# Layer passages of a two-model transformer kernel: turned input evicted ahead of the next weight rounding, and the first slot's products in the order of the input tiles

## The chip, the cores and the metric

One core of a Trainium2 chip. The metric is device time in microseconds for one launch. The kernel before took 2083.91 us, the median of three runs (2080.11 to 2088.32).

## What is computed

Two small models, one after the other, on a sequence of 512 positions of width 1024, in float32. Cut to what matters:

```python
# first model, depth 2 (layer 0: state space mixer; layer 1: sparse attention, "DSA")
x = x + mixer(rmsnorm(x, norm_mix[i]))
x = x + (silu(gate) * up) @ w_down          # gate, up = rmsnorm(x, norm_ffn[i]) @ w_gate_up, width 2816
# DSA: proj = h @ w_in; indexer scores; top 128 keys per query; softmax over them; @ w_o
# second model, depth 1
x = x + hybrid_mixer(rmsnorm(x, g_mix))     # @ w_in ("HIN"), four head groups, group norms, @ w_out ("HOUT")
x = x + cross_attention(rmsnorm(x, g_cross), rmsnorm(mem, g_mem))   # @ w_q ("XQ"), @ w_kv ("MEM"), @ w_o ("XO")
x = x + square(relu(rmsnorm(x, g_mlp) @ w_up)) @ w_down             # "MLP", width 4096
return rmsnorm(x, g_final)
```

## The kernel before

**Number format.** Every product of a layer is made of three matmuls in fp32r (`three`, L1812 to 1817): weights and inputs are split into a rounded part and a rest, and hi x hi, lo x hi, hi x lo are added. An input tile has a `xT_hi` (written by ScalarE) and a `xT_lo` (VectorE, PSUM minus hi).

**Weights** come in 147 slots of 2048 columns, in two buffers each. SP loads `raw` (`slot_free(g)` waits until slot g-2 is split), ScalarE rounds it to `w_hi` (`round_slot`, L824 to 828: waits for the load and for `w_used`, slot g-2 used up), POOL subtracts to `w_lo` (`split_rest`, L571 to 573), and TensorE waits for `w_split` before its slot.

**Two kinds of slot on TensorE.** `t_slot` (L1839) makes two output tiles of 128 columns in two PSUM banks, 2 x 8 input tiles x 3 = 48 matmuls, with the turned input as the moving operand of 512. Before, all eight input tiles go into the first output tile (then `t_first`), and all eight into the second (then `w_used`). `n_slot` (L1819) makes rows by 512 columns: four row blocks `tb` in banks 4 to 7, four input tiles each. Its user `panel` (L1910) waits for a number of `xT_lo` before each row block: 5, 6, 7, 8 where eight banks are used for turning, 4 where four are.

**Layer passages.** Between two layers the residual is finished row block by row block: VectorE adds the panel (`add_panel`), ScalarE squares, POOL makes the inverse root (`norm_rstd`), VectorE writes the left half of `x_n`, ScalarE the right half (`norm_sq`). TensorE turns `x_n` into the eight banks (`turn_normed`, L1867; bank k holds input tile k), ScalarE evicts to `xT_hi` (`turn_hi`, L815), VectorE makes `xT_lo` (`turn_lo`, L1366). The order on ScalarE is its program order: squares and `x_n`, then `round_run` of the next layer's *second* slot (L880, 898, 1085, 1143, 1153), then `turn_hi`. There are six such passages: into the first FFN (`turn_normed(0)`), DSA (1), second FFN (2), HIN (3), XQ (4) and MLP (5). `ffn_act` (L883) ends with the rounding, and `turn_hi` for DSA and HIN stands behind its call.

Where the input is not normed (WO after the DSA attention, MEM, HOUT), `turn_rows` (L1853) turns it with four banks 0 to 3: from the fifth tile on TensorE waits for the `xT_lo` four tiles back.

**Around the attention of DSA.** VectorE picks the top 128 keys (`choose_rounds`, `choose`, L1516 to 1542; each block counts up `idx_chosen`) and then starts the attention. POOL, when its head work is done, splits the first WO slot (L663) and then makes the inverse sums (`invert_sums`, L654), one per unit of attention.

## Time and profile before

| | |
|---|---|
| Median of three runs | 2083.91 us |
| The profiled execution, its time | 2082.05 us |
| Its span | 2080.20 us |
| TensorE busy | 1963.1 us (94%) |
| ScalarE, VectorE, POOL busy | 761.0, 738.5, 844.9 us (37%, 35%, 41%) |
| Mean granted TensorE clock | 0.971 |

In the profile PE is TensorE's matmuls and PEld its weight loads, DVE is VectorE, ACT ScalarE, SP the engine that issues loads. A timeline row gives the start, the time from start to end (of several instructions in a row, where x is over 1), the engine, the line, the instruction with output and inputs, and in brackets how long the engine had stood idle and what ended that. Matmuls overlap: one lasts 0.39 us while the next starts 0.227 us after it at full clock, so their spacing is read from the starts. The granted clock is in shares of 2.4 GHz; its two levels are 1.2 and 2.4 GHz, and a value between them is a stretch with both.

### The profile page before, as it was taken

How to read it: one execution, taken by the hardware profiler on the slowest of the kernel's cores; microseconds unless marked ns; L12 is line 12 of the kernel's file. 1: busy time of each engine (PE TensorE's matmuls, PEld its weight loads, DVE VectorE, ACT ScalarE, POOL GpSimd, SP SyncE). 2: the span in 40 equal slices, each digit the busy share in tenths (PEclk: the TensorE clock that was granted, in tenths of full speed). 3: DMA queues.
4: the chain of work that ended last, by engine and by line, in shares of the span. 5: the costliest groups of instructions: out<-in, count | busy, mean ns of one | idle time of the engine just before them, and what ended most of it. 6: DMA issues, size and time to landing. Idle time of an engine off the chain costs nothing.

```text
span 2080.2 us, 25333 instructions
## 1 busy us (share of the span) xinstructions
PE 1963.1 (94%) x9587; PEld 1602.7 (77%) x9587; DVE 738.5 (35%) x1279; ACT 761.0 (37%) x1233; POOL 844.9 (41%) x416
## 2 busy tenths in 40 slices
PE   2998999999998999899999999999997989999998
PEld 1777878888887878678788888878776867888887
DVE  7973231111003388852211110010158245702631
ACT  5533242322123244673332221242476353212212
POOL 1003434443444448643343443444442433443443
PEclk8799999999999899999999999999998999999999
DMA  5113323333232212101233323343300312333321
GB/s 121 18 24 127 101 81 95 87 100 91 91 101 67 81 61 82 41 22 42 81 100 101 101 80 102 103 137 95 98 22 3 110 41 70 92 102 101 100 88 75
DMA packets 210344, 168.20 MB, mean 81 GB/s; under 512 B 19537, under 2 KB 175641, under 8 KB 210200
## 3 DMA queue, kind: packets, MB, share of 16 engines
q1 hardware_dynamic: 207392, 163.10, 26.9%
q10 hardware_dynamic: 2872, 4.04, 0.6%
q8 instruction: 50, 0.82, 0.2%
q14 instruction: 30, 0.25, 0.0%
HBM read 162.63 MB, written 2.13 MB: 79 GB/s over the span
## 4 chain that ended last, share of the span: by engine, by line
PE 61%; issue 21%; POOL 8%; DVE 7%; ACT 3%; SPq 0%; DMA 0%; POOLq 0%; ACTq 0%; DVEq 0%
PE PS L1815 48%; POOL w_lo L573 7%; PE PS L1994 4%; PE PS L1978 2%; PE PS L1985 2%; ACT w_hi L828 1%; DVE stay L1591 1%; PE PS L1719 1%; PE PS L1720 1%; PE PS L1740 1%; PE PS L1752 1%; DVE o_nat L1637 0%; POOL head_rs L560 0%; DVE ranked L1526 0%; PE PS L1760 0%
## 5 line engine op out<-in xcount | busy, mean ns | idle before, releaser
L573 POOL TENSOR_TENSOR w_lo<-raw,w_hi 128x2048 fp32r<-128x2048 f32 x147 | 680.6, 4630 | 1006.7 <-ACT w_hi L828 1006.7
L828 ACT ACTIVATE w_hi<-raw 128x2048 fp32r<-128x2048 f32 x147 | 281.4, 1914 | 679.1 <-PE PS L1815 679.1
L1815 PE MATMUL PS<-xT_hi,w_hi 128*128 128x512 f32 x1104 | 432.0, 391 | 9.1 <-DVE xT_lo L1376 9.1
L1815 PE MATMUL PS<-xT_hi,w_lo 128*128 128x512 f32 x1104 | 431.7, 391 | 0.0
L1815 PE MATMUL PS<-xT_lo,w_hi 128*128 128x512 f32 x1104 | 431.4, 391 | 0.0
L1815 PEld LDWEIGHTS PS<-xT_hi,w_hi 128*128 128x128 f32 x1104 | 208.5, 189 | 53.6 <-issue 6.7
L1815 PEld LDWEIGHTS PS<-xT_lo,w_hi 128*128 128x128 f32 x1104 | 208.5, 189 | 43.6
L1815 PE MATMUL PS<-w_hi,hT_hi 128*128 128x512 f32 x608 | 237.1, 390 | 5.1 <-POOL w_lo L573 5.1
L1815 PE MATMUL PS<-w_hi,xT_hi 128*128 128x512 f32 (+2 forms) x592 | 232.3, 392 | 9.9 <-issue 4.6
L1815 PEld LDWEIGHTS PS<-xT_hi,w_lo 128*128 128x128 f32 x1104 | 208.3, 189 | 43.0
L1815 PE MATMUL PS<-w_lo,hT_hi 128*128 128x512 f32 x608 | 236.6, 389 | 0.0
L1815 PE MATMUL PS<-w_hi,hT_lo 128*128 128x512 f32 x608 | 236.6, 389 | 0.0
L1815 PE MATMUL PS<-w_hi,xT_lo 128*128 128x512 f32 (+2 forms) x592 | 230.3, 389 | 0.0
L1815 PE MATMUL PS<-w_lo,xT_hi 128*128 128x512 f32 (+2 forms) x592 | 230.2, 389 | 0.0
L1417 DVE TENSOR_TENSOR x_res<-x_res,PS 128x512 f32<-128x512 f32 x48 | 32.9, 686 | 440.8 <-PE PS L1815 440.8
L1429 DVE TENSOR_TENSOR gbuf<-gbuf,PS 128x512 f32<-128x512 f32 x44 | 30.3, 688 | 385.1 <-PE PS L1815 385.1
L1815 PEld LDWEIGHTS PS<-w_hi,xT_hi 128*128 128x128 f32 x592 | 115.8, 196 | 35.3 <-issue 9.6
L1815 PEld LDWEIGHTS PS<-w_hi,hT_hi 128*128 128x128 f32 x608 | 114.1, 188 | 30.4 <-POOL w_lo L573 6.8
L1815 PEld LDWEIGHTS PS<-w_hi,hT_lo 128*128 128x128 f32 x608 | 114.1, 188 | 23.8
L1815 PEld LDWEIGHTS PS<-w_lo,hT_hi 128*128 128x128 f32 x608 | 114.1, 188 | 23.6
L1815 PEld LDWEIGHTS PS<-w_hi,xT_lo 128*128 128x128 f32 x592 | 115.5, 195 | 21.4
L1815 PEld LDWEIGHTS PS<-w_lo,xT_hi 128*128 128x128 f32 x592 | 115.9, 196 | 20.8
(322 smaller groups left out, 2200.7 us busy)
## 6 DMA issues: line engine op xcount, KB each, us to landing
raw<-in_ffn_w_gate_up SPq DMA_DIRECT2D x88, 512.0 KB, 4.9
raw<-in_ffn_w_down SPq DMA_DIRECT2D x40, 512.0 KB, 4.5
raw<-in_w_up SPq DMA_DIRECT2D x32, 512.0 KB, 4.8
raw<-in_w_down SPq DMA_DIRECT2D x32, 512.0 KB, 4.5
raw<-in_dsa_w_in SPq DMA_DIRECT2D x28, 512.0 KB, 4.2
raw<-in_w_in SPq DMA_DIRECT2D x21, 512.0 KB, 4.2
raw<-in_s_w_glu SPq DMA_DIRECT2D x16, 512.0 KB, 4.6
raw<-in_dsa_w_o SPq DMA_DIRECT2D x8, 512.0 KB, 4.3
```

The source lines that it names most:

```text
L573: pool.tensor_tensor(w_lo[:, par, :], raw[:, par, :], f32(w_hi[:, par, :]), ALU.subtract).then_inc(w_split, 1)
L828: act.activation(w_hi[:, par, :], raw[:, par, :], ACT.Copy).then_inc(w_rounded, 1)
L1417: tt(x_res[:, tb, cols], x_res[:, tb, cols], PS[:, 4 + tb, :], ALU.add).then_inc(n_free, 1)
L1429: tt(gbuf[:, pair, 1, :], gbuf[:, pair, 0, :], PS[:, 2 * pair + 1, :], ALU.mult).then_inc(t_free, 1)
L1591: dve.tensor_tensor_scan(rest[:, ::-1], rest[:, ::-1], one[:, 0:1].broadcast_to([P, cols]), 1.0, ALU.mult, ALU.mult).then_inc(at_max, 1)
L1719: mm(o, uT[:, GB * b + g, :], taps[:, g, :, :].rearrange("p t h -> p (t h)"), start=True, stop=False)
L1720: ins = mm(o, states[:, g, :], out_a[b % 3][:, g, 1:CH + 1, :].rearrange("p t h -> p (t h)"), start=False, stop=True)
L1740: mm(o, b_n[:, GB * b + g, :], out_a[b % 3][:, g, 0:CH, :].rearrange("p t h -> p (t h)"), start=g % 4 == 0, stop=False)
L1815: ins = mm(o, a if weights_stay else c, c if weights_stay else a, start=first and n == 0, stop=last and n == 2)
L1978: mm(PS[:, t % 4, 0:k.shape[1]], q[half:half + HD], k[half:half + HD], start=True, stop=True).then_inc(at_dot, 1)
L1985: ins = tr(PS[:, 4 + e % 2, P * j:P * j + P], logit[:, e % 4, P * j:P * j + P], ident[:, :])
L1994: ins = mm(PS[:, 6 + e % 2, 0:P], probT[:, e % 2, P * j:P * j + P], v[j], start=j == 0, stop=j == len(v) - 1)
```

## The change

It has four parts.

1. ScalarE: in all six passages `turn_hi` moves ahead of the `round_run` that stood before it.
2. TensorE, `t_slot` with turned input (the first slot of each t-layer, and, since it stands in a loop, every even slot of both FFNs and of the first MLP part; also HIN's, MEM's and XQ's first): input tile by input tile into both output tiles, so `t_first` comes one step before `w_used`. XQ uses banks 0 and 1 instead of 2 and 3, and its wait for three `xT_lo` goes; MEM waits for one tile more. `turn_normed` turns the left half of the last row block before it waits for the right half.
3. TensorE, panels with turned input (DSA, WO, HOUT): a new `n_slot_turned` goes in waves: with input tile m come row blocks 0 to m-1 for that tile, and row block m for all tiles so far. WO and HOUT turn with eight banks, starting at bank 4, and HOUT's turning waits for `vx` to be evicted. DSA's passage turns and evicts tiles 4 to 7 first (`UPPER_FIRST`), and its two weight slots are loaded in that order.
4. POOL waits for `idx_chosen` 3 before it splits the first WO slot.

```diff
@@ sync
-            panel_loads(DSA_SLOT, w_in[:, :, 3 * D:3 * D + 512], 512)
+            for j, k in enumerate((4, 0)):
+                slot_free(DSA_SLOT + j)
+                load_rows((DSA_SLOT + j) % 2, w_in[:, k:k + 4, 3 * D:3 * D + 512], 512)
@@ gpsimd
+            pool.wait_ge(idx_chosen, 3)
             split_run(WO_SLOT, 1)
@@ scalar
             norm_sq(0, glu_done, 4 * TB, slice(768, D))
+            turn_hi(KT, KT, gain=2, banks=8)
             round_run(9, 1)
-            turn_hi(KT, KT, gain=2, banks=8)
...
                 norm_sq(1 + 2 * layer, n_free, TB * (FFN_PANEL[layer] + 3))
+                turn_hi((2, 5)[layer] * KT, KT, gain=(1, 4)[layer], banks=8, order=(UPPER_FIRST, range(KT))[layer])
                 round_run(g0 + FT + 1 + 2 * len(FFN_DOWN), 1)
...
             attend_act(dsa_units, DSA_UNIT, late_slot=(40, WO_SLOT + 1))
-            turn_hi(3 * KT, KT)
+            turn_hi(3 * KT, KT, banks=8, at=4)
...
-            tiles_out(XQ_SLOT, XQ_TILE, qxT, HD ** -0.5)
+            tiles_out(XQ_SLOT, XQ_TILE, qxT, HD ** -0.5, pair=0)
@@ tensor, t_slot
-                for t in range(2):
-                    for k in range(KT):
-                        if turns is not None and t == 0:
-                            pe.wait_ge(x_lo_done, turns - KT + k + 1)
-                        at = step[0] * k + step[1] * t
...
-                    ins.then_inc(w_used if t else t_first, 1)
+                for k in range(KT):
+                    pe.wait_ge(x_lo_done, turns - KT + k + 1)
+                    tile(0, k)
+                    if k == 1:
+                        tile(1, 0)
+                    if k >= 1:
+                        tile(1, k)
+            def n_slot_turned(g, par, ni, ks, j0):
+
+                pe.wait_ge(w_split, g + 1)
+                for m in range(TB):
+                    pe.wait_ge(x_lo_done, j0 + m + 1)
+                    pe.wait_ge(n_free, ni * TB + m + 1)
+                    for tb, j in [(tb, m) for tb in range(m)] + [(m, j) for j in range(m + 1)]:
+                        cols = slice(512 * j, 512 * j + 512)
+                        ins = three(PS[:, 4 + tb, :], w_hi[:, par, cols], w_lo[:, par, cols],
+                                    xT_hi[:, ks[j], P * tb:P * tb + P], xT_lo[:, ks[j], P * tb:P * tb + P], False, j == 0, False)
+                ins.then_inc(w_used, 1)
@@ tensor, turn_rows
-                    if k >= 4:
-                        pe.wait_ge(x_lo_done, j0 + k - 3)
+                    if k >= banks:
+                        pe.wait_ge(x_lo_done, j0 + k - banks + 1)
@@ tensor, turn_normed
+                for tb in range(TB - 1):
+                    left(tb)
+                pe.wait_ge(norm_right, TB * n + TB - 1)
+                for k in range(4, 7):
+                    for tb in range(TB - 1):
+                        turn(k, tb)
+                if not upper_first:
+                    left(TB - 1)
+                pe.wait_ge(norm_right, TB * n + TB)
                 for k in range(4, 7):
                     turn(k, TB - 1)
-                for t in range(TB):
-                    turn(7, t)
+                for tb in range(TB):
+                    turn(7, tb)
+                if upper_first:
+                    left(TB - 1)
@@ tensor, program
-            turn_rows(3 * KT, KT, o_nat)
-            for j in range(2):
-                panel(WO_SLOT + 2 * j, WO_PANEL + j, turns=(3 * KT, None)[j])
+            turn_rows(3 * KT, KT, o_nat, banks=8, at=4)
+            panel_turned(WO_SLOT, WO_PANEL, 3 * KT)
+            panel(WO_SLOT + 2, WO_PANEL + 1)
...
-            pe.wait_ge(x_lo_done, 6 * KT + 4 + 2 * (MEM_TILE % 2) + 1)
+            pe.wait_ge(x_lo_done, 6 * KT + 4 + 2 * (MEM_TILE % 2) + 2)
...
+            pe.wait_ge(n_free, TB * (MEM_PANEL + 2))
             pe.wait_ge(grp_norm, TB)
...
-            pe.wait_ge(x_lo_done, 8 * KT + 2 * (XQ_TILE % 2) + 1)
-            t_slot(XQ_SLOT, XQ_SLOT % 2, XQ_TILE, XQ_TILE % 2, xT_hi, xT_lo, turns=9 * KT)
+            t_slot(XQ_SLOT, XQ_SLOT % 2, XQ_TILE, 0, xT_hi, xT_lo, turns=9 * KT)
```

## Rows read from the trace of the kernel before

**Rows 1.** page, part 1: busy us of each engine (share of the span) xinstructions
```profile
PE 1963.1 (94%) x9587; PEld 1602.7 (77%) x9587; DVE 738.5 (35%) x1279; ACT 761.0 (37%) x1233; POOL 844.9 (41%) x416
```

**Rows 2.** TensorE's waits: us in total, times, longest us
```profile
PE PS L1815 <- DVE xT_lo L1376: 10.6, 5, 3.2
...
PE PS L1985 <- ACT logit L1048: 9.0, 2, 8.0
```

**Rows 3.** timeline, second FFN's passage: start us, us, engine, line, instruction [idle before]
```profile
992.59 2.40 PE L1870 MATMUL PS<-ident,x_n 128*128 128x128 f32 x20 [0.26 <-ACT x_n L854]
...
993.57 1.90 ACT L828 ACTIVATE w_hi<-raw 128x2048 fp32r<-128x2048 f32 x1
...
995.38 4.71 ACT L821 ACTIVATE xT_hi<-PS,gains 128x512 fp32r<-128x512 f32 x8
...
995.55 4.57 POOL L573 TENSOR_TENSOR w_lo<-raw,w_hi 128x2048 fp32r<-128x2048 f32 x1 [2.64 <-ACT w_hi L828]
...
996.07 5.36 DVE L1376 SCALAR_TENSOR_TENSOR xT_lo<-PS,gains,xT_hi 128x512 fp32r<-128x512 f32 x8 [2.64 <-ACT xT_hi L821]
...
996.97 0.62 PE L1815 MATMUL PS<-xT_hi,w_hi 128*128 128x512 f32 x1 [1.98 <-DVE xT_lo L1376]
...
1000.69 0.39 PE L1815 MATMUL PS<-xT_hi,w_hi 128*128 128x512 f32 x1
```

**Rows 4.** the same view, passage into DSA
```profile
641.92 0.73 ACT L854 ACTIVATE x_n<-x_res,rstd 128x512 f32<-128x512 f32 x1 [0.41 <-POOL rstd L586]
...
648.54 0.47 PE L1815 MATMUL PS<-w_hi,xT_hi 128*128 128x512 f32 x1 [4.57 <-issue]
```

**Rows 5.** the same view, passage into the WO panel
```profile
942.36 1.73 PEld L1859 LDWEIGHTS PS<-ident,o_nat 128*128 128x128 f32 x16 [0.57 <-DVE o_nat L1608]
...
946.63 0.48 PE L1815 MATMUL PS<-w_hi,xT_hi 128*128 128x512 f32 x1
```

**Rows 6.** the same view, passages into first FFN, HIN, HOUT (two), XQ and MLP
```profile
271.85 5.28 PE L1870 MATMUL PS<-ident,x_n 128*128 128x128 f32 x24 [0.62 <-DVE x_n L1386]
...
1367.63 0.47 PE L1815 MATMUL PS<-xT_hi,w_hi 128*128 128x512 f32 x1 [1.99 <-DVE xT_lo L1376]
...
1611.61 4.21 PEld L1859 LDWEIGHTS PS<-ident,o_nat 128*128 128x128 f32 x24 [3.45 <-issue]
...
1617.16 0.48 PE L1815 MATMUL PS<-w_hi,xT_hi 128*128 128x512 f32 x1
...
1668.73 0.50 PE L1815 MATMUL PS<-xT_hi,w_hi 128*128 128x512 f32 x1 [3.20 <-DVE xT_lo L1376]
...
1718.43 2.81 PE L1870 MATMUL PS<-ident,x_n 128*128 128x128 f32 x24 [0.93 <-DVE x_n L1386]
```

**Rows 7.** the same view, end of top-k and start of the attention
```profile
845.40 4.51 POOL L573 TENSOR_TENSOR w_lo<-raw,w_hi 128x2048 fp32r<-128x2048 f32 x1
...
845.79 4.40 DVE L1535 TENSOR_SCALAR ranked<-score,top 128x512 f32<-128x512 f32 x1
...
850.95 0.49 DVE L1537 TENSOR_SCALAR equal<-score,top 128x512 f32<-128x512 f32 x1
...
856.12 2.08 POOL L661 TENSOR_TENSOR inv_sum<-row_sum,minus_one 128x1 f32<-128x1 f32 x4 [6.22 <-ACT logit L1048]
...
858.24 0.28 DVE L1608 TENSOR_SCALAR o_nat<-PS,inv_sum 128x64 f32<-128x64 f32 x1 [0.48 <-PE PS L1994]
```

**Rows 8.** the same view, XO slot: first and last of 24 matmuls
```profile
1710.84 0.39 PE L1815 MATMUL PS<-w_hi,xT_hi 128*128 128x512 f32 x1
...
1716.06 0.39 PE L1815 MATMUL PS<-w_hi,xT_lo 128*128 128x512 f32 x1
```

**Rows 9.** stretches: us, busy us of five engines (x), PEclk (granted clock), DMA, GB/s
```profile
995.00:1000.00 5.00, 3.03 (x8) 2.40 (x9) 3.93 (x6) 5.00 (x9) 4.45 (x1) 0.71 0.01 3
...
1367.00:1372.00 5.00, 4.37 (x19) 3.67 (x20) 5.00 (x8) 3.74 (x7) 3.80 (x1) 1.00 0.02 3
```

**Rows 10.** one line's instructions: duration ns min/median/max, first and last start us, form
```profile
L1637 DVE TENSOR_TENSOR o_nat<-o_nat,rstd x4: 1219/1223/5592, 1602.5 to 1605.9; 128x1024 f32<-128x1024 f32 x4
```

More of the change, by code:

```diff
@@ L813, in _, with turn_hi @@
             states_out(NB - 1)
-            def turn_hi(j0, n, gain=None, width=S, dst=xT_hi, view=None, banks=4, k0=0):
-                for k in range(k0, n):
-                    act.wait_ge(turned, j0 + k + 1)
-                    o, i = dst[:, k, 0:width], PS[:, k % banks, 0:width]
+            def turn_hi(j0, n, gain=None, width=S, dst=xT_hi, view=None, banks=4, k0=0, order=range(KT), at=0):
+                for n_th in range(k0, n):
+                    k = order[n_th]
+                    act.wait_ge(turned, j0 + n_th + 1)
+                    o, i = dst[:, k, 0:width], PS[:, (k + at) % banks, 0:width]
                     if view:
@@ L1364, in _, with turn_lo @@
                     output_map(b + 2)
-            def turn_lo(j0, n, gain=None, width=S, hi=xT_hi, lo=xT_lo, view=None, banks=4):
-                for k in range(n):
-                    dve.wait_ge(x_hi_done, j0 + k + 1)
-                    o, h, i = lo[:, k, 0:width], f32(hi[:, k, 0:width]), PS[:, k % banks, 0:width]
+            def turn_lo(j0, n, gain=None, width=S, hi=xT_hi, lo=xT_lo, view=None, banks=4, order=range(KT), at=0):
+                for n_th in range(n):
+                    k = order[n_th]
+                    dve.wait_ge(x_hi_done, j0 + n_th + 1)
+                    o, h, i = lo[:, k, 0:width], f32(hi[:, k, 0:width]), PS[:, (k + at) % banks, 0:width]
                     if view:
@@ L1440, in _ @@
             ffn_dve(0)
-            turn_lo(2 * KT, KT, gain=1, banks=8)
+            turn_lo(2 * KT, KT, gain=1, banks=8, order=UPPER_FIRST)
             dve.wait_ge(ld_qk, 16 * 4)
@@ L1853, in turn_rows, with tile @@
-            def turn_rows(j0, n, src, tbs=TB):
+                def tile(t, k):
+                    at = step[0] * k + step[1] * t
+                    cols = slice(at, at + P)
+                    ins = three(PS[:, 2 * pair + t, 0:width], w_hi[:, par, cols], w_lo[:, par, cols],
+                                hi[:, k, 0:width], lo[:, k, 0:width], True, k == 0, k == KT - 1)
+                    if k == KT - 1:
+                        ins.then_inc(w_used if t else t_first, 1)
+                if turns is None:
+                    for t in range(2):
+                        for k in range(KT):
+                            tile(t, k)
+                    return
@@ L1872, in turn, with left @@
                         ins.then_inc(turned, 1)
-                for tb in range(TB):
+                def left(tb):
                     pe.wait_ge(norm_left, TB * n + tb + 1)
@@ L1906, in _, with panel, panel_turned @@
             ffn_pe(0, 2 * KT)
-            turn_normed(1, 2 * KT)
-            def panel(g0, ni, n=512, turns=None, banks=4, after=None):
+            turn_normed(1, upper_first=True)
+            def panel(g0, ni, n=512, after=None):
                 for k in range(2):
-                    need = [turns + min(KT, (4 + 4 * k if banks == 4 else 5 + tb + 4 * k)) for tb in range(TB)] if turns is not None else None
-                    n_slot(g0 + k, (g0 + k) % 2, ni, range(4 * k, 4 * k + 4), xT_hi, xT_lo, k == 0, k == 1, n, turns=need, after=after)
+                    n_slot(g0 + k, (g0 + k) % 2, ni, range(4 * k, 4 * k + 4), xT_hi, xT_lo, k == 0, k == 1, n, after=after)
+            def panel_turned(g0, ni, j0, order=range(KT)):
+                n_slot_turned(g0, g0 % 2, ni, order[0:4], j0)
+                n_slot(g0 + 1, (g0 + 1) % 2, ni, order[4:KT], xT_hi, xT_lo, False, True, turns=[j0 + KT] * TB)
             def turn_heads(pi):
```

51 lines of the change are left out of this document (22 added, 29 removed).

## The prediction

> **What bounds the kernel now.** I read the page first: TensorE is busy 94% of the span, no other engine over 41% [rows 1]. The layers' inner loops are therefore bound by matmuls, which the change leaves alone. Time can only come from the holes in TensorE's row. The list of its waits shows which holes the change touches: five waits for `xT_lo`, together 10.6 us, and one of 8.0 us for the first softmax exponent [rows 2]. Then I read the timeline of each layer passage, since the list hides what stood behind each wait.
>
> Rows 3 are the pattern (the passage into the second FFN). TensorE turns the last block of rows, 20 transposes from 992.59 in 2.40 us. ScalarE meanwhile rounds the *next* weight slot (`w_hi`, 1.90 us), and only at 995.38 begins to evict the turned tiles. VectorE follows at 996.07 with `xT_lo`, 8 tiles in 5.36 us or 0.67 each, and TensorE starts at 996.97 on the first one. The rounded slot is needed one whole slot later: 48 matmuls of 0.227 us, 10.9 us. So the 1.9 us rounding stands on the path for nothing.
>
> **The change, part by part.**
>
> *Eviction ahead of rounding.* In `turn_normed` the left half of row block 3 now comes straight after nine upper transposes. Spacing is 0.11 (2.40 = 19 x 0.11 + 0.3), so its first transpose starts at 992.59 + 9 x 0.11 = 993.6 and is in PSUM at 993.9. ScalarE is free from 993.6 [rows 3]. Eviction then starts at 993.9 instead of 995.38 and TensorE at 995.5 instead of 996.97: **1.45 us**. The later tiles don't break this: they arrive every 0.67 us, and a step of three matmuls takes 0.68 us, of which two per tile are now issued. HIN (start 1367.63 [rows 6]) has the same rows: **1.45**. At MLP the 24 transposes begin late, at 1718.43, and take 2.81 [rows 6], so the first turned tile is there about 0.1 later: **1.35**. At the first FFN the 24 transposes take 5.28 us from 271.85 [rows 6], until 277.1, at 0.22 spacing: the transposes themselves end last, and the gain is **0** (bounds 0 and 0.2).
>
> *XQ* gains the same 1.45. It also waited for the third `xT_lo`, because its outputs lay in banks 2 and 3, and now needs one: two tiles of 0.67 more, **2.8** in all, from a wait shown as 3.20 [rows 6].
>
> *DSA.* TensorE starts at 648.54 [rows 4], since the old order wants five `xT_lo` tiles for its first row block. Now the upper four are turned and evicted first, which frees banks 4 to 7, and the first product needs one tile. ScalarE's last `x_n` ends at 642.65 [rows 4]; one transpose and its landing later, at 643.05, eviction starts; as in rows 3, VectorE follows 0.69 later (996.07 - 995.38) and TensorE 0.90 after that (996.97 - 996.07): 644.65. **3.9 us.** The waves of 1, 3, 5 and 7 products take 0.68 each, longer than the 0.67 to the next tile, so no wave waits.
>
> *WO and HOUT.* All eight tiles have banks of their own, so TensorE turns 32 blocks without waiting. WO: 16 took 1.73, 0.108 each [rows 5]; 32 end at 942.36 + 3.5 = 945.85 against a start at 946.63: **0.75**. HOUT: 24 took 4.21 from 1611.61, part of them at low clock, and eight more end about 1616.5 against 1617.16 [rows 6]: **0.65** (0.4 to 0.8). The new wait for `vx` stands before a longer one for `grp_norm` and costs nothing. The memory slot waits for one more `xT_lo`, 0.4 us, inside that same wait.
>
> *What is paid.* The rounding that was moved ends eight evictions later: in rows 3 the evictions take 4.71 from 993.9, rounding 1.9, POOL's split 4.57, in all 1005.1. TensorE wants that slot at 995.5 + 10.9 = 1006.4. Cover left: 1.3 us (0.9 at DSA). Behind the split stands SP's load of slot g+3, 5 us later, wanted only after slot g+1 is finished; nothing there. The interleaved order puts `t_first` 0.68 us before the slot's end instead of 5.4: ScalarE's first output (0.6 us) still ends before the second can be read, and each PSUM pair has a slot of 10.9 us to come free. At DSA VectorE makes the rope tables right after the tiles, now beside POOL's split, and may be held up to that split's 4.6 us; POOL reads `qk_tables` before the third slot's split, and the panel that the tables serve ends two slots of 10.9 us after the start. Cost 0.
>
> *The bank order.* Interleaving switches the PSUM bank every three matmuls instead of every 24: about 12 more switches in each of 29 slots (11 in each FFN, 4 in the MLP, HIN, MEM, XQ) and 5 in each of three panels, 363. The nearest rows are the second half of the XO slot, 24 matmuls with a switch every six: starts 1710.84 to 1716.06, 5.22 / 23 = 0.227 [rows 8], the spacing inside one bank. I take 0; by the rounding of these rows the bound is 0.005 us a switch, 2 us in all, either way.
> The Trainium skill speaks against this order ("TensorE: Matmul & The Clock Gate", A second HAM failure mode): a kernel that cycled PSUM banks lost throughput by micro-idles and an oscillating clock. It gives no price here; the trace doesn't agree at a switch every six, and no row has one every three. By that rule the change would end slower (rival C).
>
> *The held split.* POOL splits WO's slot from 845.40 to 849.9. VectorE's compare of SBUF with a scalar, issued at 845.79, takes 4.40 us; the next of its shape takes 0.49 [rows 7]. It stands on the top-k chain for which the attention waits (8.0 us [rows 2]). Held back until the choice is made, this gives 3.9. But the split now comes before the first inverse sum on POOL's queue. The choice ended about 1 us before the first inverse sum (856.12 [rows 7]); shifted by 3.9 it ends at 851.2, and the first scaling, 858.24 [rows 7], would come at 854.3. POOL splits until 855.8, the first inverse (0.52, four took 2.08) is there at 856.3: 2.1 us late. The units behind it overlap, so a little is won back, and TensorE's clock stays low a little longer. Bounds of the net: 0.8 and 3.9; I take **2.0**, near the plain difference of 1.8.
>
> *The clock.* After the hole in rows 3 the matmuls start 0.43 apart: nine take 996.97 to 1000.69, 3.72 instead of 2.04, a loss of 1.7. The granted clock of that stretch is 0.71 [rows 9], a mixture of 1.2 and 2.4 GHz. Of the five passages with a hole of 2 to 4.6 us, four show this (DSA, the second FFN, XQ, MLP); HIN doesn't, at the same 2.0 us [rows 6, 9]. WO, with no hole over 0.4, doesn't either. With holes near 0.6 us I expect one of the five to fall instead of four: 3 x 1.6 = **4.8**, bounds 0 and 6.4.
>
> **Sum.** 1.45 + 1.45 + 1.35 + 2.8 + 3.9 + 0.75 + 0.65 = 12.35 at the starts, + 2.0 + 4.8 = 19.15. The profiled execution took 2082.05 (span 2080.20): 2062.9. It lay 1.86 under the median of the three runs, so I forecast 2065.
>
> **The rivals.**
> A, the clock still falls as before: only the starts move, 14.35: 2069.5. For it: HIN and the second FFN had equal holes and behaved differently, and transposes go on for five microseconds ahead of either. Against: WO. Chance 0.17.
> B, the cover is too thin: the moved split ends after TensorE wants it. It decides when the evictions, rounding and split together slip 1.3 us. A slip of 2.5 costs 1.2 in each of five passages and keeps four of them in a hole, so the clock gain goes too: 19.15 - 6 - 4.8 = 8.3 left, 2075.5. Against: none of the three waits for anything else, and where the clock falls TensorE's slot gets longer too. Chance 0.06.
> C, slower: the bank switch every three matmuls. It decides at 19.15 / 363 = 0.053 us each; at 0.08 it takes 29 us and the kernel ends at 2094. For it only the page; against it rows 8. Chance 0.06.
> D, the change doesn't move the starts because something else in the passage ends last (TensorE's own transposes, as at the first FFN): 2080, chance 0.05.
> E, more than forecast: the hold gives its full 3.9, no fall is left, and at HOUT VectorE's last `o_nat` scaling, 5.59 us long beside a split where the others take 1.22 [rows 10], slips out in front of it (up to 2.8, since TensorE is then late with its own panel): 2057 to 2060. Chance 0.08.
>
> **How the numbers follow.** The forecast has 0.58, and with its own bounds runs 2060 to 2069. The range 2057 to 2073 takes in A and E and the 4 us by which the runs themselves lie on either side of their median; it leaves B, C, D and the tails out. Within 0.5%, about what a measurement of this kernel can tell from no change, is a gain under 10.4, above 2073.5. Faster by more: the forecast, A and E nearly whole, 0.81. Same: B, D and bad tails, 0.13. Slower: C, 0.06.
>
> **What would show it.** In the changed profile: ScalarE's `xT_hi` follows the last `x_n` within 0.4 us and `w_hi` follows the eighth `xT_hi`; TensorE's wait for `xT_lo` falls from 10.6 to about 4; in DSA the first matmul comes about 2 us after the last `x_n`; VectorE's compare takes 0.49; matmuls of the first slots are 0.227 apart, three and three in two banks. I am wrong if TensorE then waits for `w_lo` at the second slot of a layer, if the spacing at a bank switch is wider, or if the first scaling after the choice comes over 6 us late.

## The result and the profile after

The changed kernel took **2061.78 us** (median of 4 runs, 2059.70 to 2063.56) against 2085.45 us (4 runs, 2080.11 to 2088.32) for the kernel before beside it: ratio **0.9889**, 95% interval 0.9865 to 0.9913. The forecast was 2065 (2057 to 2073), faster. The profiled execution took 2063.24 us, span 2061.4, against 2082.05 and 2080.2. In the changed code `three` is L1819, `turn_normed` L1899, `turn_rows` L1888, `turn_hi` L827, `turn_lo` L1380, the rounding L834, POOL's split L577.

Page, part 1, and TensorE's waits (us in total, times, longest us), for [rows 1, 2]:

```profile
PE 1958.1 (95%) x9587; PEld 1598.4 (78%) x9587; DVE 738.5 (36%) x1279; ACT 761.0 (37%) x1233; POOL 844.1 (41%) x416
```
```profile
PE PS L1819 <- POOL w_lo L577: 8.1, 5, 3.0
...
PE PS L2024 <- ACT logit L1054: 5.1, 2, 4.1
...
PE PS L1819 <- DVE xT_lo L1380: 3.8, 5, 1.6
```

The wait for `xT_lo` fell from 10.6 to 3.8, that for the first exponent from 8.0 to 4.1, and `w_lo` (8.2 before) didn't grow: no moved split came too late. TensorE's busy time fell by 5 us for the same 9587 matmuls; the work is the same, so this is mostly the clock.

The passage into the second FFN, timeline, for [rows 3]:

```profile
986.57 2.40 PE L1899 MATMUL PS<-ident,x_n 128*128 128x128 f32 x20 [0.31 <-ACT x_n L860]
986.93 0.72 ACT L860 ACTIVATE x_n<-x_res,rstd 128x512 f32<-128x512 f32 x1 [0.41 <-POOL rstd L590]
...
987.92 4.73 ACT L827 ACTIVATE xT_hi<-PS,gains 128x512 fp32r<-128x512 f32 x8 [0.27 <-PE PS L1899]
988.64 5.36 DVE L1380 SCALAR_TENSOR_TENSOR xT_lo<-PS,gains,xT_hi 128x512 fp32r<-128x512 f32 x8 [1.22 <-ACT xT_hi L827]
989.54 0.47 PE L1819 MATMUL PS<-xT_hi,w_hi 128*128 128x512 f32 x1 [0.56 <-DVE xT_lo L1380]
...
991.66 0.39 PE L1819 MATMUL PS<-xT_hi,w_hi 128*128 128x512 f32 x1
...
992.49 1.96 ACT L834 ACTIVATE w_hi<-raw 128x2048 fp32r<-128x2048 f32 x1
...
994.53 4.60 POOL L577 TENSOR_TENSOR w_lo<-raw,w_hi 128x2048 fp32r<-128x2048 f32 x1 [7.64 <-ACT w_hi L834]
```

ScalarE evicts 0.27 us after its last `x_n`, TensorE's hole is 0.56 us instead of 1.98, and nine matmuls later it is at 991.66: 2.12 us instead of 3.72, full clock from the start. The split ends at 999.13; TensorE wants it at 989.54 + 10.9 = 1000.4.

DSA ([rows 4]), then HOUT's transposes ([rows 6]) and the end of top-k with the attention's start ([rows 7]):

```profile
643.57 0.72 ACT L860 ACTIVATE x_n<-x_res,rstd 128x512 f32<-128x512 f32 x1 [0.41 <-POOL rstd L590]
...
644.71 4.73 ACT L827 ACTIVATE xT_hi<-PS,gains 128x512 fp32r<-128x512 f32 x8 [0.42 <-PE PS L1899]
...
646.28 0.47 PE L1819 MATMUL PS<-w_hi,xT_hi 128*128 128x512 f32 x1 [0.52 <-issue]
...
841.59 0.49 DVE L1539 TENSOR_SCALAR ranked<-score,top 128x512 f32<-128x512 f32 x1
...
847.09 4.51 POOL L577 TENSOR_TENSOR w_lo<-raw,w_hi 128x2048 fp32r<-128x2048 f32 x1 [5.88 <-DVE chosen L1546]
...
851.56 2.08 POOL L665 TENSOR_TENSOR inv_sum<-row_sum,minus_one 128x1 f32<-128x1 f32 x4
...
852.21 0.28 DVE L1612 TENSOR_SCALAR o_nat<-PS,inv_sum 128x64 f32<-128x64 f32 x1 [2.57 <-POOL inv_sum L665]
...
1603.80 3.68 PE L1888 MATMUL PS<-ident,o_nat 128*128 128x128 f32 x32 [2.91 <-DVE o_nat L1641]
```

The compare takes 0.49 instead of 4.40, and the first scaling then waits 2.57 us for POOL's inverse sum, which stands behind the split that was held.

**Stretch by stretch**, from first matmul to first matmul, worked out from the starts in the timelines (us; "again" are the second traces of experiments `f0_before` and `c0_changed`; the attention begins with its first turned probabilities, L2024):

| stretch | before | before, again | changed | changed, again |
|---|---|---|---|---|
| start to first FFN | 276.85 | 278.00 | 278.57 | 277.85 |
| to DSA | 371.69 | 371.64 | 367.71 | 367.88 |
| to the attention | 207.66 | 207.62 | 201.79 | 205.31 |
| to WO's transposes | 86.17 | 86.13 | 89.06 | 89.14 |
| to WO's first matmul | 4.27 | 4.27 | 3.47 | 3.47 |
| to the second FFN | 50.34 | 50.34 | 48.93 | 48.92 |
| to HIN | 370.66 | 370.65 | 367.59 | 367.60 |
| to HOUT's transposes | 244.02 | 248.28 | 246.68 | 246.67 |
| to HOUT's first matmul | 5.52 | 6.28 | 3.44 | 6.35 |
| to XQ | 51.56 | 51.54 | 48.92 | 48.92 |
| to MLP | 54.40 | 55.67 | 49.82 | 49.80 |
| to the end | 357.09 | 355.46 | 355.46 | 355.49 |

Most stretches repeat to 0.1 us. Where the granted clock was low for longer in one of two executions of one program they don't: to the attention by 3.5 us (both changed), to HOUT's transposes by 4.3 (both before), HOUT by 2.9 (both changed), the start to the first FFN by 0.7 and 1.2, and the last two rows of the kernel before by 1.3 and 1.6. The experiments are read by stretches for that reason, and the whole time is used only for effects above some 5 us.

### The profile page after: what moved, and what is told of

The parts are those of the page before. It is cut to its first block, busy times and chain, and to the rows that moved or that the text cites. A ratio compares the mean times of both kernels' runs of the same rounds, so it can differ in the third digit from the quotient of the medians.

```text
span 2061.4 us, 25321 instructions
## 1 busy us (share of the span) xinstructions
PE 1958.1 (95%) x9587; PEld 1598.4 (78%) x9587; DVE 738.5 (36%) x1279; ACT 761.0 (37%) x1233; POOL 844.1 (41%) x416
## 4 chain that ended last, share of the span: by engine, by line
PE 62%; issue 20%; POOL 8%; DVE 7%; ACT 2%; SPq 0%; DMA 0%; POOLq 0%; ACTq 0%; DVEq 0%
PE PS L1819 48%; POOL w_lo L577 7%; PE PS L2033 4%; PE PS L2017 2%; PE PS L2024 2%; DVE stay L1595 1%; PE PS L1723 1%; PE PS L1724 1%; PE PS L1744 1%; PE PS L1756 1%; ACT w_hi L834 0%; DVE o_nat L1641 0%; POOL head_rs L564 0%; DVE ranked L1530 0%; PE PS L1764 0%
## 5 line engine op out<-in xcount | busy, mean ns | idle before, releaser
L577 POOL TENSOR_TENSOR w_lo<-raw,w_hi 128x2048 fp32r<-128x2048 f32 x147 | 680.0, 4626 | 1005.9 <-ACT w_hi L834 1000.0
L834 ACT ACTIVATE w_hi<-raw 128x2048 fp32r<-128x2048 f32 x147 | 281.8, 1917 | 566.8 <-PE PS L1819 565.0
L1819 PE MATMUL PS<-xT_hi,w_hi 128*128 128x512 f32 x1104 | 430.0, 390 | 2.3 <-DVE xT_lo L1380 2.3
L1819 PE MATMUL PS<-xT_lo,w_hi 128*128 128x512 f32 x1104 | 429.5, 389 | 0.0
L1819 PE MATMUL PS<-xT_hi,w_lo 128*128 128x512 f32 x1104 | 429.5, 389 | 0.0
L1819 PEld LDWEIGHTS PS<-xT_hi,w_hi 128*128 128x128 f32 x1104 | 207.2, 188 | 46.2 <-issue 3.3
L1819 PE MATMUL PS<-w_hi,hT_hi 128*128 128x512 f32 x608 | 237.0, 390 | 5.1 <-POOL w_lo L577 5.1
L1819 PEld LDWEIGHTS PS<-xT_lo,w_hi 128*128 128x128 f32 x1104 | 207.3, 188 | 43.2
L1819 PEld LDWEIGHTS PS<-xT_hi,w_lo 128*128 128x128 f32 x1104 | 207.3, 188 | 42.6
L1819 PE MATMUL PS<-w_lo,hT_hi 128*128 128x512 f32 x608 | 236.6, 389 | 0.0
L1819 PE MATMUL PS<-w_hi,hT_lo 128*128 128x512 f32 x608 | 236.6, 389 | 0.0
L1819 PE MATMUL PS<-w_hi,xT_hi 128*128 128x512 f32 (+2 forms) x592 | 230.2, 389 | 5.8 <-POOL w_lo L577 3.0
L1819 PE MATMUL PS<-w_hi,xT_lo 128*128 128x512 f32 (+2 forms) x592 | 228.2, 386 | 0.0
L1819 PE MATMUL PS<-w_lo,xT_hi 128*128 128x512 f32 (+2 forms) x592 | 228.2, 385 | 0.0
L1819 PEld LDWEIGHTS PS<-w_hi,xT_hi 128*128 128x128 f32 x592 | 114.0, 193 | 31.0 <-issue 5.5
L1819 PEld LDWEIGHTS PS<-w_hi,hT_hi 128*128 128x128 f32 x608 | 114.1, 188 | 30.3 <-POOL w_lo L577 6.8
L1819 PEld LDWEIGHTS PS<-w_hi,hT_lo 128*128 128x128 f32 x608 | 114.1, 188 | 23.8
L1819 PEld LDWEIGHTS PS<-w_lo,hT_hi 128*128 128x128 f32 x608 | 114.1, 188 | 23.7
L1819 PEld LDWEIGHTS PS<-w_hi,xT_lo 128*128 128x128 f32 x592 | 114.0, 193 | 21.1
L1819 PEld LDWEIGHTS PS<-w_lo,xT_hi 128*128 128x128 f32 x592 | 114.2, 193 | 20.5
```

The source lines that it names most:

```text
L577: pool.tensor_tensor(w_lo[:, par, :], raw[:, par, :], f32(w_hi[:, par, :]), ALU.subtract).then_inc(w_split, 1)
L834: act.activation(w_hi[:, par, :], raw[:, par, :], ACT.Copy).then_inc(w_rounded, 1)
L1819: ins = mm(o, a if weights_stay else c, c if weights_stay else a, start=first and n == 0, stop=last and n == 2)
```

## The experiments

Theory: the starts, as summed; the clock, since short holes no longer bring it down; the hold, minus what it gives back. Rivals as in the prediction.

### The same two kernels once more

`f0_before` is the kernel before, `c0_changed` the changed one, both unaltered.

> The kernel before, once more and unaltered, for a second trace of it: passages of the same length as in the first (6.6 us from ScalarE's last x_n to the first matmul at DSA, 4.03 at the second FFN, HIN and MLP, 5.25 at XQ). Theory (the low stretches behind a passage come from its hole, in most but not all cases): three to five of these five passages, and the stretch behind XQ's attention, have one again, not all at the places of the first trace. Rival (chance that has nothing to do with the holes): none to two, or as many in the fillings between the passages.

> The changed kernel once more, unaltered, beside the others on the same chip: 2062, ratio to the kernel before 0.990. What repeats and what does not: the lengths of the passages (from the last x_n of ScalarE to the first matmul: 2.72 at DSA, 2.61 at the second FFN, HIN and XQ, 2.65 at MLP) should come out the same to 0.05; the stretches from HIN's first matmul to HOUT's first transpose (244.1 or 246.7 in the profiles so far), from DSA's first matmul to the attention (201.8 or 205.4) and HOUT's own (3.44, 5.0 or 6.3) should take one of these values each, since they go with low stretches of the clock that come and go.

Measured: 1.0006 (0.9996 to 1.0017) and 0.9912 (0.9895 to 0.9929; 2066.59 us). The second trace of before has lowered clock behind DSA, second FFN, HIN and XQ, and not behind MLP; the first had it behind DSA, second FFN, XQ and MLP, not behind HIN. Four of five both times, at other places, as the theory has it. Stretches of five us from near the first matmul on in `f0_before`, in the columns of [rows 9] (PEclk stands after the engines): second FFN, HIN.

```profile
998.00:1003.00 5.00, 5.00 (x15) 4.00 (x16) 4.46 (x7) 4.40 (x7) 3.15 (x1) 0.66 0.08 23
1369.00:1374.00 5.00, 5.00 (x16) 3.95 (x15) 4.12 (x7) 2.77 (x5) 2.81 (x1) 0.66 0.13 32
```

In `c0_changed` none of the five has it. But HOUT's 32 transposes, 3.68 us long in the first changed trace, take 6.59 in this one, partly at 0.5, behind the same wait of 2.91:

```profile
1606.84 6.59 PE L1888 MATMUL PS<-ident,o_nat 128*128 128x128 f32 x32 [2.91 <-DVE o_nat L1641]
```

### The order on ScalarE undone, and in doses

```diff
-            turn_hi(KT, KT, gain=2, banks=8)
             round_run(9, 1)
+            turn_hi(KT, KT, gain=2, banks=8)
```

`b1_round_first` does this in all six passages, `h1_xq_only` in the one into XQ. `g1_half` puts half of the rounding in front (columns 0 to 1023) and half behind, `g2_double` rounds twice in front.

> The changed kernel with the order on ScalarE undone in all six passages: the next slot is rounded before the turned tiles are evicted. Theory (the prediction's): the first matmul of the second FFN, HIN, XQ and MLP comes 1.4 us later each and DSA's 1.9 later, 7.5 in all, and the clock falls again behind four of the five holes, 1.6 each: 14 slower, about 2076. Rival A (the falls of the clock don't hang on the length of these holes): 7.5 slower, about 2069, with about as many low stretches behind the passages as the changed kernel has, which is none. Rival D (the first matmul waits for something else): under 2 slower.

> The changed kernel, but ScalarE rounds one half of the next slot in front of the eviction and the other half behind it, in all six passages: a hole that is 0.5 us longer (half a rounding is 0.97; the first 0.48 of a whole one was hidden, since the whole one moves the first matmul by 1.42). Theory: 0.5 later in each of four passages and 0.3 at DSA, 2.3 in all; at a hole of about 1.1 us the clock still falls nowhere behind these five: 2.3 slower. Rival: the falls grow with the hole, one or two of five: 4 to 5.5 slower.

> The changed kernel, but ScalarE rounds the next slot twice in front of the eviction (the second time over the same values): 1.42 + 1.95 = 3.4 us later in the second FFN, HIN, XQ and MLP, 3.2 at DSA, 16.8 in all. Theory (a longer hole makes the fall surer): the clock falls behind all five passages, 1.65 each, 8.3: 25 slower than the changed kernel, about 2087 and slower than the kernel before. Rival A (the falls don't hang on the length of the hole, two of five as with one rounding): 20 slower, about 2082. Rival B (the moved weights become the bound: the rounding ends so late that TensorE waits for w_lo at the second slot): a new wait for w_lo and over 28 slower.

> The changed kernel with the order on ScalarE undone in one passage only, the one into XQ: the hole there is 2.0 us again and the other passages keep 0.6. Question: in every trace with longer holes (two of the kernel before, one and two roundings in front) the clock has a low stretch 27 to 37 us behind XQ's first matmul, in work that the change doesn't touch, and in none with short holes. Theory (the hole in front of XQ is what brings it): from HOUT's first matmul to XQ's 50.3 us instead of 48.9, and from XQ's first to MLP's 51.5 instead of 49.8, with a low stretch in it; 3.1 slower than the changed kernel in these two stretches. Rival 1 (the hole only moves the start): 1.4 slower, 50.3 and 49.8. Rival 2 (it comes from the other holes, or from the place in time of the whole part): as rival 1 here. The whole time can't tell, 2063 to 2068 in any case; the trace decides.

First matmul of the second FFN, in b1, g1 and g2:

```profile
992.57 0.47 PE L1819 MATMUL PS<-xT_hi,w_hi 128*128 128x512 f32 x1 [1.99 <-DVE xT_lo L1380]
```
```profile
990.85 0.47 PE L1833 MATMUL PS<-xT_hi,w_hi 128*128 128x512 f32 x1 [1.13 <-DVE xT_lo L1394]
```
```profile
999.74 0.77 PE L1835 MATMUL PS<-xT_hi,w_hi 128*128 128x512 f32 x1 [3.93 <-DVE xT_lo L1396]
```

The same stretches behind it, in the same order of kernels (PEclk 0.66, 1.00, 0.52):

```profile
993.00:998.00 5.00, 5.00 (x17) 3.91 (x16) 4.03 (x7) 3.97 (x6) 2.71 (x1) 0.66 0.18 43
```
```profile
991.00:996.00 5.00, 5.00 (x23) 4.08 (x24) 4.31 (x7) 4.98 (x8) 1.01 (x1) 1.00 0.01 3
```
```profile
1000.00:1005.00 5.00, 5.00 (x13) 3.90 (x13) 4.20 (x7) 4.14 (x6) 2.87 (x1) 0.52 0.11 32
```

*b1*: ratio 0.9963 (0.9953 to 0.9973), 2073.70 us; against the two ratios of the changed kernel, 0.9889 and 0.9912, that is 11 to 15 us more, which alone doesn't tell the theories apart. DSA starts 1.26 later, second FFN, HIN and XQ 1.42, MLP 1.38: 6.9, near the 7.5 of both theories. The clock falls behind one passage (second FFN) and once in XQ's attention, 1.6 each: 10.1 in all, where the theory said 14 and rival A 7.5. So one rounding in front leaves a hole behind which the clock falls sometimes, here once in five.

*g1*: 2063.90 us, 0.9913 (0.9896 to 0.9929). Starts 0.42 to 0.57 later, 2.6 in all (2.3 said), and no fall: the theory, not its rival.

*g2*: 2092.88 us, 1.0054 (1.0037 to 1.0070), slower than the kernel before. Four starts come 3.3 to 3.4 later and DSA's 3.2, as said, and the clock falls behind all five, behind the second FFN and MLP at a cost of 2.4 and 2.9 us instead of 1.6. The expectation, 25 slower than the changed kernel, was too low: the trace is 29.5 longer than the first changed one. It had left out the first FFN, whose transposes no longer cover two roundings (1.8), the two longer falls, and a fall in XQ's attention (1.6). No wait for `w_lo` appeared, so rival B falls even there (8.2 us, five times, as before).

*h1*: HOUT to XQ 50.35, XQ to MLP 51.42, the two numbers of the theory (50.3, 51.5). But the low stretch isn't where I had asked for it: it stands directly behind the hole, and the later place is at full clock:

```profile
1658.00:1663.00 5.00, 4.83 (x14) 3.87 (x15) 4.63 (x8) 3.28 (x6) 3.32 (x1) 0.66 0.04 10
...
1692.00:1698.00 6.00, 4.89 (x21) 4.05 (x22) 2.91 (x5) 3.47 (x6) 3.90 (x1) 1.00 0.00 0
```

The hole costs 1.4 + 1.6 there. What brings the low stretch that begins 34 to 37 us behind XQ's start is open: it is in both traces of before, in b1 and in g2, and in none of the ten others. The median, 2072.00 (2066.84 to 2075.77; ratio 0.9951, 0.9929 to 0.9974), lies above the 2063 to 2068 that I had expected, and the one trace, with a span of 2065.0, doesn't show why.

**All passages together** (DSA, second FFN, HIN, XQ, MLP in 14 traces). Hole in front of the first matmul 0.5 to 0.6 us: 43 cases, no lowered clock. 0.9 to 1.1 us: 5 cases, none. 1.8 to 2.5 us: 13 cases, 6 with it. Above 3 us: 9 cases, 9 with it.

### Parts of the new order on TensorE

`b2_tile_by_tile` undoes the interleaving in `t_slot`, `e1_no_waves` the waves in `n_slot_turned`:

```diff
-                for k in range(KT):
-                    pe.wait_ge(x_lo_done, turns - KT + k + 1)
-                    tile(0, k)
-                    if k == 1:
-                        tile(1, 0)
-                    if k >= 1:
-                        tile(1, k)
+                for t in range(2):
+                    for k in range(KT):
+                        if t == 0:
+                            pe.wait_ge(x_lo_done, turns - KT + k + 1)
+                        tile(t, k)
...
-                    pe.wait_ge(x_lo_done, j0 + m + 1)
+                    pe.wait_ge(x_lo_done, j0 + TB)
...
-                    for tb, j in [(tb, m) for tb in range(m)] + [(m, j) for j in range(m + 1)]:
+                    for tb, j in [(m, j) for j in range(TB)]:
```

> The changed kernel, but in its slots with turned input all eight input tiles go into the first output tile and then into the second, as before (one bank for 24 matmuls instead of a switch every three). Theory (the switch is free, and the order pays only where a tile arrives later than TensorE asks for it; tiles come 0.67 us apart and three matmuls take 0.68): within 0.5 us of the changed kernel, with no new wait for xT_lo. Rival C (a bank switch costs): faster, by 15 us if a switch costs 0.04. Rival: without the second product per tile TensorE waits for xT_lo again between tiles, 0.2 to 0.5 us in each of five layers, which with the clock comes to 2 to 8 slower.

> The changed kernel, but the first slot of the three panels with turned input (DSA, WO, HOUT) goes row block by row block again and waits for its four xT_lo tiles; the order of turning and all banks stay. Theory (a row block needs four tiles, three more than the wave, 0.67 each): DSA's first matmul comes 2.0 later (4.7 behind ScalarE's last x_n instead of 2.72), WO's about 0.3 and HOUT's about 0.3 later, and with a hole of that length the clock falls once more, 1.6: 2.6 slower without and 4.2 with it. Rival (TensorE gains nothing by starting early, since it is then held at the later tiles): under 0.5 slower.

*b2*: 2066.33 us, 0.9919 (0.9899 to 0.9938). Every stretch agrees with `c0_changed` to 0.1 us (second FFN to HIN 367.63, HOUT to XQ 48.92, MLP to end 355.45), and the wait for `xT_lo` is 3.8 us, five times, as in the changed kernel. The interleaving earns nothing and costs nothing: what shortens the passages of the two-tile slots is ScalarE's order alone, and at XQ the banks too.

*e1*: 2064.64 us, 0.9907 (0.9893 to 0.9922). DSA's first matmul comes 4.69 us behind the last `x_n` instead of 2.72, so the waves are worth 1.97 there (the first slot's 48 matmuls take 10.97 us with the waves and 11.00 without, so the early start isn't lost to later waits), WO's 0.44. HOUT's first matmul follows at 5.11, as in b1 and g2 with the waves: the 0.3 expected there isn't seen. The hole of 2.49 us in front of DSA brought no fall this time:

```profile
649.00:654.00 5.00, 4.50 (x20) 3.74 (x21) 4.93 (x8) 3.49 (x4) 1.43 (x1) 1.00 0.00 0
```

**What each part is worth at the starts**, from ScalarE's last `x_n` to the first matmul. At the second FFN and HIN b1 brings back the 4.03 of the kernel before, so the 1.42 hang on ScalarE's order. XQ: 5.25 before, 4.03 in b1, 2.60 changed: 1.4 for the order and 1.2 for the banks with their shorter wait. DSA: 6.62 before, 2.72 changed: 1.26 for the order (b1), 1.97 for the waves (e1), and 0.67 left, which falls to turning the upper tiles first. WO: 0.44 for the waves and 0.36 left for the eight banks. What is left over is a difference, not a run. The edit to `turn_normed`, outside DSA, is worth nothing: the old code too turned the left half of the last row block straight after the nine upper transposes and before it waited for the right half, and at the second FFN the last 20 transposes start 0.35 and 0.36 us before the last `x_n` and run 2.40 us (before, changed). Only two earlier waits fell away.

### The price of a bank switch

`c1_switch_each` lets TensorE go to the other output bank at every matmul in the two-tile slots that take their input whole:

```diff
                 if turns is None:
-                    for t in range(2):
-                        for k in range(KT):
-                            tile(t, k)
+                    for k in range(KT):
+                        at = [step[0] * k, step[0] * k + step[1]]
+                        for n in range(3):
+                            for t in range(2):
+                                wt = (w_hi, w_lo, w_hi)[n][:, par, at[t]:at[t] + P]
+                                x = (hi, hi, lo)[n][:, k, 0:width]
+                                ins = mm(PS[:, 2 * pair + t, 0:width], wt, x, start=k == 0 and n == 0, stop=k == KT - 1 and n == 2)
                                if k == KT - 1 and n == 2:
                                    ins.then_inc(w_used if t else t_first, 1)
```

> The changed kernel, but in the 41 slots of two output tiles that take their input whole, TensorE switches between the two PSUM banks at every matmul (47 switches a slot where there was 1: 1886 more). Theory (a switch is free): spacing stays 0.227, time within 1 us of the changed kernel, 2062. Rival C (a switch costs): at 0.005 each 9 us slower, 2071; at 0.053, from which the change would have gained nothing, 100 us slower.

First and last of the 24 pairs of one such slot, a row being one pair:

```profile
309.76 0.62 PE L1863 MATMUL PS<-xT_hi,w_hi 128*128 128x512 f32 x2
...
320.18 0.62 PE L1863 MATMUL PS<-xT_lo,w_hi 128*128 128x512 f32 x2
```

10.42 / 23 = 0.453 a pair, 0.2265 a matmul, the spacing inside one bank. The second FFN's stretch, with 11 such slots and 506 more switches, is 367.90 against 367.60: at most 0.0006 us a switch. Rival C is out. The section "A second HAM failure mode" of the Trainium skill ("TensorE: Matmul & The Clock Gate") tells of a kernel that cycled through PSUM banks and whose clock oscillated because TensorE idled briefly between groups of matmuls. This trace doesn't show it: in the second FFN's stretch the clock stayed at its high level with 506 more switches, and the spacing stayed at 0.2265 us. Alternating banks is then not enough by itself; the idle times of that section didn't arise here, so its own cause isn't tested.

The kernel as a whole took 2058.56 us, 0.9882 (0.9867 to 0.9896), 8 under `c0_changed`, which none of the theories said, and 3 under the changed kernel's first median, 2061.78, whose ratio 0.9889 it can't be told from. In the traces the 10 us between the two lie in the stretches that don't repeat: to the attention 200.50 against 205.31, to HOUT's transposes 243.99 against 246.67, HOUT 5.02 against 6.35, the attention 88.34 against 89.14. Only seven slots of HIN among these contain switches. I read it as the clock's luck and not as a gain of the switching: the changed kernel itself came once at 2061.78 (ratio 0.9889) and once at 2066.59 (0.9912). It wasn't tested further.

### The two splits on POOL

`a0_after_again` (in spite of its label not the changed kernel) takes the hold away. `a2_split_in_attention` moves WO's split behind the 24th inverse sum, and `d1_both` does that and the same for HOUT's.

```diff
-            pool.wait_ge(idx_chosen, 3)
-            split_run(WO_SLOT, 1)
-            invert_sums(dsa_units, DSA_UNIT, 0, 40)
+            invert_sums(dsa_units, DSA_UNIT, 0, 24)
+            split_run(WO_SLOT, 1)
+            invert_sums(dsa_units, DSA_UNIT, 24, 40)
...
+            pool.wait_ge(grp_norm, TB)
             split_run(MEM_SLOT + 2, 2)
```

> The changed kernel with its fourth part undone: POOL no longer waits for the choice before it splits the first WO slot. Theory (the prediction's net of 2.0 for the hold): 2.0 us slower than the changed kernel, about 2064; VectorE's compare takes 4.4 us again instead of 0.49, the attention's first matmul comes 3.9 us later after DSA's first, and the attention itself, from its first matmul to the first turning transpose behind it, takes 87.2 us again instead of 90.1. Rival 1 (the two profiles read against each other: 3.9 gained in front, 2.9 given back inside): 1.0 slower. Rival 2 (nothing is given back, the longer attention of the changed profile is chance): 3.9 slower, and the attention stays at 90.1 without the hold as well.

> The changed kernel, but POOL splits the first WO slot behind the 24th inverse sum of the attention instead of in front of the first; the wait for the choice goes, since the sums themselves come after it. Theory (what the hold gives back is the split in front of the first inverse sum): compare 0.49, the first scaling about 3.1 us behind the attention's first matmul instead of 5.2, the attention 87.2 us long, 2.9 faster than the changed kernel, about 2059. Rival 1: the low clock at the attention's start belongs to the hole in front of it, not to the split: the first scaling is early but the attention stays near 90, gain under 1. Rival 2: the split in the middle holds up a unit itself, a wait of up to 4.5 us for inv_sum near the 24th unit, gain 0 or below.

> The changed kernel with two splits of POOL moved: WO's first slot behind the 24th inverse sum, and HOUT's first slot behind the four scalings of o_nat by VectorE. Theory (both splits lengthen a VectorE or POOL step on TensorE's path): attention 86.1 instead of 89.1 from its first matmul to the first transpose behind it; the last scaling takes 1.22 instead of 5.61, so the transposes into HOUT start when vx is evicted, 2.7 earlier, and TensorE's first matmul follows 3.44 behind. 5.7 faster than the changed kernel, about 2056. Rival (the split, now started 2.2 later, is what TensorE waits for): HOUT's first matmul comes 4.5 to 5 behind its first transpose, gain there 1 to 1.5, whole 4.

In the kernel without the hold the compare is long again, and the first scaling comes 2.05 us behind the first turned probabilities instead of 4.14:

```profile
838.37 4.51 POOL L577 TENSOR_TENSOR w_lo<-raw,w_hi 128x2048 fp32r<-128x2048 f32 x1
838.79 4.37 DVE L1538 TENSOR_SCALAR ranked<-score,top 128x512 f32<-128x512 f32 x1
```

| | compare | to the attention | attention | whole time, ratio |
|---|---|---|---|---|
| changed, changed again | 0.49 | 201.79, 205.31 | 89.06, 89.14 | 0.9889, 0.9912 |
| without the hold | 4.37 | 205.75 | 86.94 | 0.9909 (0.9893 to 0.9924) |
| WO's split in the attention | 0.49 | 205.40 | 86.09 | 0.9911 (0.9893 to 0.9928) |
| both splits moved | 0.49 | 205.24 | 87.18 | 0.9867 (0.9852 to 0.9881) |

The hold gains 3.9 in front (4.37 - 0.49). The whole stretch to the attention hides this, since it also holds low stretches of the clock; from the last compare's start to the first turned probabilities it is 10.37 to 10.40 us in the three traces with the long compare (the two of before and a0) and 6.48 or 6.49 in the other eleven. With its split in front of the first inverse sum the hold gives 2.1 (89.06 - 86.94) to 2.9 (89.06 - 86.17) back inside: net 1.0 to 1.8 between these traces, so rival 2 of a0 is out, and the whole time can't tell the 2.0 from the 1.0.

Over all traces the attention took 88.3 to 90.4 us in the nine with the split in front of the first sum, and 86.1 to 87.2 in the five without. The granted clock parts this in two. TensorE stood at the low level for 8.4 to 14.7 us of the attention in the nine, and for 4.0 to 7.3 in the five; between traces of the same order the attention is 0.32 us longer for each such us (a2 to d1: 1.10 for 3.32; c1 to g1: 2.03 for 6.36). So of the 2.9 between the profiled pair (4.4 us low before, 10.6 changed) I estimate 2.0 for the clock and 0.9 for the wait itself. Why the clock stays low longer behind the split in front wasn't tested.

With the split behind the 24th sum the attention is 3.0 shorter than in `c0_changed`, and TensorE waits for no `inv_sum`: the theory of a2 holds for its stretch. In the whole time, where it said 2059, the median came at 2063.06 and shows no gain. Ten us at its start, from a2 and then from the changed kernel, run at 0.78 and 0.50:

```profile
850.00:860.00 10.00, 9.48 (x55) 6.76 (x55) 6.41 (x36) 7.99 (x38) 6.75 (x13) 0.78 0.01 2
```
```profile
847.00:857.00 10.00, 8.24 (x35) 5.90 (x35) 4.63 (x27) 5.84 (x27) 9.11 (x10) 0.50 0.32 105
```

In `d1_both` the four scalings of `o_nat` take 4.6 us together instead of 9.03, and TensorE no longer waits for them (group of L1642; transposes and first matmul):

```profile
L1642 DVE TENSOR_TENSOR o_nat<-o_nat,rstd 128x1024 f32<-128x1024 f32 x4 | 4.6, 1220 | 4.8 <-POOL rstd L564 4.8
```
```profile
1599.63 3.68 PE L1889 MATMUL PS<-ident,o_nat 128*128 128x128 f32 x32 [0.58 <-issue]
...
1603.08 0.48 PE L1820 MATMUL PS<-w_hi,xT_hi 128*128 128x512 f32 x1
```

HIN to HOUT's transposes is 241.70, 2.3 under the lowest of the others (2.7 said), and HOUT's first matmul follows 3.44 behind: the later split isn't waited for. The attention, 86.1 expected, took 87.19, with more of it at the low clock than in a2 (7.3 us against 4.0). **2055.86 us** (2054.31 to 2059.16) against 2066.59 for the changed kernel beside it, with intervals that don't meet (0.9852 to 0.9881 and 0.9895 to 0.9929): `d1_both` beats the kernel before, and the changed kernel as measured beside it. The whole time doesn't carry the second: c1, which saves no work, is only 2.7 us slower. The two stretches do. Of the 10 us between these two traces, 2.0 + 2.3 belong to the moved splits; the rest is clock, 2.7 in front of HOUT's transposes and 2.9 in them. The missing wait isn't needed for that: the first changed trace and a2 have the wait of 2.9 us and the same 3.44.

Both long instructions fit a rule of the Trainium skill ("SBUF — State Buffer", Who interferes with whom): VectorE and GpSimd share a port pair, held for a whole instruction, and the later one blocks. The traces agree: 4.37 for 0.49 here and 5.61 for 1.22 in the changed kernel, each issued while a split ran and ended 0.3 and 1.1 us behind the split's end. The changed kernel's pair:

```profile
1597.44 5.13 POOL L577 TENSOR_TENSOR w_lo<-raw,w_hi 128x2048 fp32r<-128x2048 f32 x1 [2.85 <-ACT w_hi L834]
1598.04 5.61 DVE L1641 TENSOR_TENSOR o_nat<-o_nat,rstd 128x1024 f32<-128x1024 f32 x1
```

## Why the prediction was right

| term | forecast | profiled pair |
|---|---|---|
| first FFN | 0 | 0.2 |
| DSA | 3.9 | 3.90 |
| WO | 0.75 | 0.80 |
| second FFN, HIN | 1.45 each | 1.41, 1.42 |
| XQ | 2.8 | 2.65 |
| MLP | 1.35 | 1.38 |
| HOUT | 0.65 | 2.08; 0.5 or 0 at equal clock |
| hold, net | 2.0 | 1.0 (3.9 less 2.9) |
| clock behind the five passages | 4.8 | 6.5, and 2.0 further on |
| stretches elsewhere | 0 | -4.6 |

**The starts** were right to 0.2 each, in all 12.3 against 12.35 if HOUT is taken at 0.5: rows of the same engines in the same kernel (0.67 a tile, 0.11 a transpose, 0.9 from `xT_lo` to TensorE) carry such a sum. HOUT's 5.52 to 3.44 holds the end of a low stretch; where both have one of equal size (5.02 in a0, c1 and g1) the order is worth 0.5. Where it is longer, in `f0_before` (6.28) and h1 (6.27), the order is worth nothing, so HOUT's 0.65 stands on one comparison only. MEM's edits cost nothing, as said: HIN to HOUT's transposes takes 244.02 before and 244.07 in a0, where no extra low stretch lies in it.

**The cover** held: `w_lo` was waited for no more than before. Rival B is out, and in g2 even two roundings didn't reach it.

**The eviction's start** had a reason too many: "now comes straight after nine upper transposes" describes the old order as well (992.59 and 986.57, 20 transposes, 2.40 us each time). The sum is right because it took the moment when the first tile is in PSUM, which the change leaves alone, and let ScalarE begin there.

**The interleaving** wasn't needed. The prediction counted two products per tile as a safeguard for the later tiles, but its own numbers, a tile every 0.67 us and 0.68 for three matmuls, already said that one product per tile is enough; b2 shows it.

**The hold** was mis-sized: 2.1 us late was right to 0.1 (the first scaling came at 4.14 instead of 2.05 behind the first turned probabilities), but "a little is won back" was wrong. The attention came out 2.9 longer than before, of which about 2.0 is the longer time at the low clock, the other half of that same sentence. Other pairs of traces give 2.1, so the net of 2.0 was too high by 0.2 to 1.0.

**The clock** was mis-sized as a term: 8.5 instead of 4.8. The clock fell behind none of the five passages, where I had left one; the four falls that went cost 1.6 each, as read. One more in XQ's attention (1.6), which I hadn't counted, went too, and 0.4 lies between DSA's first slots and the attention. "One of the five" was a guess from two kinds of holes, 0.4 and 2.0; in the doses no fall stands behind a hole of up to 1.1, and the shortest hole with one is 1.9.

**What made the sum come out** at 18.8 of 19.15: the two errors (+3.7, -1.0) and HOUT's luck (+1.6) were met by -4.6 in places that the change doesn't touch: 1.9 before the first FFN and 2.7 between HIN and HOUT. That they met was luck; another pair of traces would have summed otherwise. In the medians the change brought 23.7 at first and, by the ratio of `c0_changed`, 18; the interval of either holds the forecast. Rivals A, C and D are out. E was right in its clock and wrong in its hold; the long scaling at HOUT that it named was still there (5.61 us), and d1 is the edit that takes it away.

## What to carry to other kernels

Look at what an engine does between the last input and the first consumer of a passage: work that is wanted a whole slot later belongs behind it, and its cost is read off two rows. A split or copy on POOL should stand where VectorE's dependent chain is not, and ahead of no small instruction that someone waits for; holding it back is only half the move. When two traces of one program differ by more than the effect, compare stretches between fixed points, and take a second trace of the kernel before.

## What the runs showed of the hardware

Behind none of the 48 holes of up to 1.1 us did the granted clock fall, behind 6 of the 13 of 1.8 to 2.5, and behind all 9 of 3.2 to 4.6. Equal holes in the same passage went either way (HIN, 1.99 and 1.98 us, in the two traces of the kernel before), so a single trace doesn't tell what a hole of 2 us costs. A fall took 1.6 us more from the matmuls behind it in twelve cases and 2.4 to 2.9 in three.

Low stretches come and go elsewhere too. `b2_tile_by_tile` and `c0_changed`, whose passages start within 0.1 us of each other all along, have the same twelve stretches to 0.1 us, lowered ones included; `c1_switch_each`, whose first FFN starts 0.9 us earlier, has others, and its trace is 10 us shorter. That the starting times decide it is a guess from these three. What is shown is the size: two traces of the unaltered changed kernel differ by 6 us in span, so a few us of whole time are no evidence for an edit.

A change of PSUM bank between matmuls cost nothing that could be measured: 0.0006 us at most in the second FFN (506 more switches), and nothing from MLP to the end (552 more, 355.44 us against 355.46 and 355.49).

A VectorE instruction issued while POOL split a weight slot ended only behind the split: 4.37 us instead of 0.49 for a compare, 5.61 instead of 1.22 for a scaling of 1024 columns.
